# Two mixing blocks on one core: attention with fused maximum, transform in bin pairs, third filter layer kept in SBUF, output projection begun with the gating rows

## The reference

```python
# block 1: 8 query heads of 64, 2 key heads, band of 128 tokens to either side
h = rmsnorm(x, g); q, k, v, g_a, u_p, g_p = split(h @ w_in)
s = where(valid, (q @ k.T) * 64**-0.5 + bias, -1e30)
m = maximum(max(s), sink); p = exp(s - m); p = p / (sum(p) + exp(sink - m))
a = (p @ v) * silu(g_a); p = multiscale_pool(u_p, pool_w) * silu(g_p)
x = x + rmsnorm(concat([a, p]) @ w_out, post_g)
# block 2: a long convolution and a gated spatial unit
h = rms_norm(x, w); hy_in, hy_gate, sg_u, sg_v, sg_gate = split(h @ w_in)
x0, x1, v = split(short_conv(hy_in)); k = hyena_filter(...)  # 3 sine layers, decay, divided by its absolute sum
y_a = x0 * (irfft(rfft(v * x1) * rfft(k)) + v * x1 * skip) * silu(hy_gate)
y_b = spatial_gate(sg_u, sg_v) * silu(sg_gate)
x = x + rms_norm(concat([y_a, y_b]) @ w_out, post_w)
```

## Time and profile before

| | us |
|---|---|
| median of three runs | 3576.2 |
| the profiled execution, its own time | 3573.78 |
| its span in the profile | 3572.0 |
| PE busy | 3248.9 (91%) |
| DVE busy | 2550.0 (71%) |
| ACT busy | 731.7 (20%) |

### The profile page before, as it was taken

The page is one execution under the profiler, slowest core; times in us unless marked ns, Lnnn a source line. Parts: engine busy times, 40 slices in busy tenths (PEclk is TensorE's granted clock), DMA queues, the critical chain, the costliest instruction groups (busy, mean ns, idle before and its releaser), DMA issues. The chain is left out here.

```text
span 3572.0 us, 33998 instructions
## 1 busy us (share of the span) xinstructions
PE 3248.9 (91%) x13506; PEld 2287.5 (64%) x13506; DVE 2550.0 (71%) x2615; ACT 731.7 (20%) x1267; POOL 316.8 (9%) x420
## 2 busy tenths in 40 slices
PE   6999999999995789999999999996798989859999
PEld 3444445664444668777788887874465656657887
DVE  6999993995993687999999999942465656443221
ACT  2000001662221220000111111112342433222110
POOL 3222210001330450000000000000000000000010
PEclk9999999999997999999999999998899999969999
DMA  6555542002448454566455554313102020135331
GB/s 200 146 155 141 145 108 95 7 1 89 155 151 277 157 150 127 158 156 177 144 136 141 139 139 139 99 33 146 49 1 98 13 83 18 65 118 165 94 95 59
DMA packets 210784, 407.99 MB, mean 114 GB/s; under 512 B 20657, under 2 KB 132465, under 8 KB 202561
## 3 DMA queue, kind: packets, MB, share of 16 engines
q1 hardware_dynamic: 190720, 335.00, 30.7%
q0 software_dynamic: 18752, 62.42, 6.8%
q10 hardware_dynamic: 1152, 8.39, 0.6%
HBM read 318.70 MB, written 87.05 MB: 114 GB/s over the span
## 5 line engine op out<-in xcount | busy, mean ns | idle before, releaser
L1535 PE MATMUL PS<-HH,WH 128*128 128x512 f32 x1536 | 607.8, 396 | 35.9 <-DVE WL L1433 16.6
L1537 PE MATMUL PS<-HH,WL 128*128 128x512 f32 x1536 | 604.9, 394 | 0.0
L1536 PE MATMUL PS<-HL,WH 128*128 128x512 f32 x1536 | 600.8, 391 | 0.0
L730 PE MATMUL PS<-M 128*128 128x512 f32 x1152 | 498.9, 595 | 6.3 <-DVE M L567 3.7
L97 DVE SCALAR_TENSOR_TENSOR MF<-MF 128x1024 f32<-128x1024 f32 x315 | 404.2, 1283 | 10.0
L730 PEld LDWEIGHTS PS<-M 128*128 128x128 f32 x1152 | 219.5, 191 | 285.1 <-issue 279.0
L1535 PEld LDWEIGHTS PS<-HH,WH 128*128 128x128 f32 x1536 | 290.4, 189 | 102.8 <-DVE MB L1469 14.1
L1537 PEld LDWEIGHTS PS<-HH,WL 128*128 128x128 f32 x1536 | 289.9, 189 | 65.7
L1536 PEld LDWEIGHTS PS<-HL,WH 128*128 128x128 f32 x1536 | 290.1, 189 | 64.3
L1979 PE MATMUL PS<-M 128*128 128x256 f32 x1024 | 260.0, 398 | 14.1 <-DVE M L1870 8.5
L1979 PEld LDWEIGHTS PS<-M 128*128 128x128 f32 x1024 | 190.8, 191 | 71.2 <-issue 24.9
(11 more groups left out here) (190 smaller groups left out, 4628.0 us busy)
## 6 DMA issues: line engine op xcount, KB each, us to landing
MF<-h_scratch SPq DMA_DIRECT2D x380, 256.0 KB, 4.3
M<-c_feat POOLq DMA_DIRECT2D x194, 256.0 KB, 4.2
MF<-w_in SPq DMA_DIRECT2D x56, 512.0 KB, 4.9
M<-u_scratch SPq DMA_DIRECT2D x16, 1024.0 KB, 4.8
M<-w_in SPq DMA_DIRECT2D x18, 512.0 KB, 5.2
M<-x SPq DMA_DIRECT2D x16, 512.0 KB, 5.5
x_scratch<-M SPq DMA_DIRECT2D x16, 512.0 KB, 2.6
h2h_scratch<-HTH SPq DMA_DIRECT2D x16, 512.0 KB, 2.7
```

The source lines that it names most:

```text
L730: ins = t.matmul(PS[:, banks + c, :], wt[:, k], HT[:, k, TC * c:TC * c + TC], start=(k == 0), stop=(k == KD - 1))
L1535: t.matmul(dst, wh, hh, start=(k == 0), stop=False)
L1536: t.matmul(dst, wh, hl, start=False, stop=False)
L1537: ins = t.matmul(dst, wl, hh, start=False, stop=(k == KD - 1))
```

## The change

In attention the scale moves into the copy of q. Addition of the bias and maximum, the sink's included, become one fused DVE instruction for each of four heads, which order shows as an ISA row and an accumulator read. PE's order becomes: two turns, the value products of the step before (now 256 columns wide, the two halves of the columns in alternation), two turns, the scores. The gate is done a step later. In the mixing loop ACT does the scaling of L658, and 17 of the first layer's operations move ahead of attention. The third layer stays in SBUF (`HP`), its sine is taken on ACT during the second last tiles, constants of the first chunk are loaded ahead, and the second block no longer ends with waits for stores. In the transform a pair of bins is one unit: two matmuls for the inputs and four for the filter in place of eight, three ACT copies, and one DVE product of 1024 columns and one difference of 512. Buffers for decay, absolute values and `GX` are double; the sums come one piece later. Banks 0 to 5 hold the pairs, 6 the inverse, 7 the next filter pieces. The last channel group has its own buffer for `GU`, and `output` starts with rows 8 to 15, whose features and first three weight rows have been loaded before the convolution ends.

```diff
-                    s.activation(Q[:, g], flat, ACT.Copy).then_inc(proj_evac, 1)
+                    s.activation(Q[:, g], flat, ACT.Copy, scale=SCALE).then_inc(proj_evac, 1)
                 elif kind == "k":
...
+                    if st >= 2:
+                        s.wait_ge(pv_done, st - 1)
+                    nk = P * len(keys_of(n))
+                    s.activation(turned_keys(st % 2, r, nk), PS[:, 4 + r % 2, 0:nk], ACT.Copy).then_inc(pT_read, 1)
...
+                s.wait_ge(x1rstd_done, i + 1)
+                s.activation(HS[:, i % 2], X1[:, i % 2], ACT.Copy, scale=RS2[:, i:i + 1]).then_inc(hs_done, 1)
...
-                link_to(v.scalar_tensor_tensor(out=sc, in0=PS[:, 0:4, c0:c1], scalar=SCALE,
-                                               in1=BIAS[:, 4 * g:4 * g + 4, c0:c1], op0=ALU.mult, op1=ALU.add),
-                        scores_read, st + 1)
-                link(v.tensor_reduce(sm[:, 0], sc, AX_X, ALU.max))
-                link(v.tensor_tensor(sm[:, 0], sm[:, 0], SINK[:, 4 * g:4 * g + 4], ALU.max))
+                for r in range(4):
+                    ins = v.tensor_tensor_reduce(out=sc[:, r], in0=PS[:, r, c0:c1], in1=BIAS[:, 4 * g + r, c0:c1], scale=1.0,
+                                                 scalar=SINK[:, 4 * g + r:4 * g + r + 1], op0=ALU.add, op1=ALU.max,
+                                                 accum_out=sm[:, 0, r:r + 1])
+                link_to(ins, scores_read, st + 1)
...
-                if st:
-                    gate(st - 1)
+                if st >= 2:
+                    gate(st - 2)
+            gate(len(STEPS) - 2)
             gate(len(STEPS) - 1)
...
-                first_layer_work(6 if i < 8 else 5)
+                first_layer_work(5 if i < 7 else 4)
...
+                if st:
+                    products(st - 1)
+                turned(2)
+                turned(3)
                 if st + 3 < len(STEPS):
                     scores(st + 3)
+            def products(st):
+                n, g = STEPS[st]
+                ks = keys_of(n)
+                t.wait_ge(pT_read, 4 * st + 4)
                 if st >= 2:
                     t.wait_ge(attn_done, st - 1)
-                product(0)
-                turned(2)
-                product(1)
-                turned(3)
-                product(2)
-                product(3).then_inc(pv_done, 1)
+                for x, kb in enumerate(ks):
+                    for odd in range(2):
+                        ins = t.matmul(PS[HD * odd:HD * odd + HD, 6 + st % 2, 0:2 * P].rearrange("p (a b) -> p a b", b=P),
+                                       V[:, kb, HD * g:HD * g + HD], turned_probs(st % 2, odd, x), start=(x == 0),
+                                       stop=(x == len(ks) - 1))
+                ins.then_inc(pv_done, 1)
             scores(0)
             scores(1)
             scores(2)
             for st in range(len(STEPS)):
                 values(st)
+            products(len(STEPS) - 1)
...
+                for d in range(2):
+                    sp.dma_start(CC[HID * d:HID * d + HID, 0:CH], A["filt_w_out_2"][:, D * d:D * d + CH]).then_inc(kept.first_in, 16)
+                sp.dma_start(CC[:, CH:2 * CH], A["c_delta"][0:CH].partition_broadcast(P)).then_inc(kept.first_in, 16)
+                sp.dma_start(CC[:, 2 * CH:], A["c_tneg"]).then_inc(kept.first_in, 16)
                 a = sum(SV_OPS)
...
-                sp.wait_ge(sin3_done, 1)
-                sp.dma_start(h3_d, L3[2]).then_inc(h3_stored, 16)
-                sp.wait_ge(h3_stored, 16)
-                for b in range(2):
-                    sp.wait_ge(yb_stored[b], 64)
-                sp.wait_ge(gx_stored, 128)
-                sp.wait_ge(u_stored, 128)
...
+                    if (kind, n) == ("hgate", 7):
+                        s.wait_ge(arg3_done, 2)
+                        s.activation(L3[2][0:HID], L3[1][0:HID], ACT.Sin).then_inc(sin3_done, 1)
+                        s.activation(L3[2][HID:P, 1:S], L3[1][HID:P, S - 1:0:-1], ACT.Sin).then_inc(sin3_done, 1)
...
+        DEC = [region(22528 + 512 * i, 512) for i in range(2)]
+        KABS = [region(23552 + 512 * i, 512) for i in range(2)]
...
+        GX = region(37888, 2, S // 2)
...
+        LAST = 2 * NCH - 1
+        GX_LAST = region_of(HP, 0, 2, S // 2)
...
+                if ug == LAST:
+                    sp.wait_ge(utr_done, 4 * LAST + 4)
+                elif ug:
+                    sp.wait_ge(ya_stored[(ug - 1) % 2], 16 * ((ug + 1) // 2))
...
-            sp.dma_start(H3[0:HID], h3_d[0:HID]).then_inc(h3_in, 16)
+                if ug == LAST:
+                    sp.wait_ge(kgen_done, 16 * NCH)
+                elif n >= 2:
+                    sp.wait_ge(gx_used, n - 1)
+                sp.dma_start(gate_part(n), gx_d[ug][:, 1024 * half:1024 * half + 1024]).then_inc(gx_last_in if ug == LAST else gx_in[half], 16)
...
+            sp.wait_ge(ia_done, 4 * (LAST - 1))
+            for b in range(2):
+                sp.wait_ge(kept.yb_stored[b], 64)
+            late_features(sp, YR, yb_d, 1, 0, kept.y_in)
+            late_weights(sp, A, WR, 0, kept.wo_in)
+            late_features(sp, YR, yb_d, 1, 1, kept.y_in)
+            for n in range(1, W_SLOTS):
+                late_weights(sp, A, WR, n, kept.wo_in)
+            sp.dma_start(GP, A["post_norm_w_2"].partition_broadcast(P)).then_inc(kept.gp_in, 16)
+            gated_out(LAST - 1)
+            gated_out(LAST)
+            sp.wait_ge(ya_stored[0], 16 * NCH)
...
-                    s.activation(DEC[:, CH * x:CH * x + CH], DELTA[:, cc % 2], ACT.Exp,
+                    s.activation(DEC[kq % 2][:, CH * x:CH * x + CH], DELTA[cc % 2], ACT.Exp,
...
+                    if 15 * cc + j > 2:
+                        s.wait_ge(kabs_added, 15 * cc + max(j - 2, 0))
+                    s.activation(KABS[j % 2], out, ACT.Abs).then_inc(kabs_done, 1)
...
-                s.activation(UTB[:, n % 16], PS[:, 4 + n % 2, :].rearrange("p (y c) -> p y c", y=2), ACT.Copy).then_inc(z_done, 1)
...
             for kq in range(16):
-                decays(kq)
+                if kq < 15:
+                    decays(kq + 1)
                 absolute(kq)
...
+                for p in range(16):
+                    n = 16 * cc + p
+                    bank = 3 * (n % 2)
+                    s.wait_ge(uk_done, n + 1)
+                    if n >= 2:
+                        s.wait_ge(pm_done, n - 1)
+                    for to in range(2):
+                        s.activation(KS[HID * to:HID * to + HID, n % 2, :, CH:2 * CH],
+                                     PS[HID - HID * to:P - HID * to, bank:bank + 2, 0:CH], ACT.Copy).then_inc(ks_done, 1)
+                    if p == 0:
+                        s.wait_ge(ks_done, ks_count(n) - 2)
+                        s.activation(KS[0:1, n % 2, 0, CH:2 * CH], PS[HID:HID + 1, bank, 0:CH], ACT.Copy,
+                                     scale=-1.0).then_inc(ks_done, 1)
+                    s.wait_ge(b_done, n + 1)
+                    s.activation(KS[:, n % 2, :, 0:CH], PS[:, bank + 2, :].rearrange("p (y c) -> p y c", y=2),
+                                 ACT.Copy).then_inc(ks_done, 1)
+                    if cc + 1 < NCH:
+                        decays(n + 16)
+                    if p:
+                        inverse_out(n - 1)
+                        if cc + 1 < NCH:
+                            absolute(n + 15)
...
+                v.tensor_tensor(out.rearrange("p (c x) -> p x c", x=2), PS[:, sample_bank(kq), :].rearrange("p (x c) -> p x c", x=2),
+                                DEC[kq % 2].rearrange("p (x c) -> p x c", x=2), ALU.mult).then_inc(k_weighted, 1)
...
+                    if n:
+                        v.wait_ge(y_done, n)
+                    v.tensor_tensor(PM, PS[:, bank:bank + 2, :], KS[:, n % 2], ALU.mult).then_inc(pm_done, 1)
+                    v.wait_ge(pm_done, n + 1)
+                    v.tensor_tensor(UTB[:, p], PM[:, :, 0:CH], PM[:, :, CH:2 * CH], ALU.subtract).then_inc(y_done, 1)
+                    if cc + 1 < NCH:
+                        weighted(n + 16)
+                        if p >= 2:
+                            summed(n + 14)
...
+                if kq >= 16:
+                    t.wait_ge(k_weighted, kq)
+                elif kq >= 2:
...
                 bp = n % 16
-                t.wait_ge(y_done, 2 * n + 2)
-                if n >= 2:
-                    t.wait_ge(z_done, n - 1)
...
-                    for m, (strip, which) in enumerate(FORMS):
-                        src = (UTB if which == "u" else KTB[cc % 2])[:, b // 2, b % 2]
-                        ins = t.matmul(PS[:, 2 * (bb % 2) + m // 2, CH * (m % 2):CH * (m % 2) + CH],
-                                       STRIP[:, b, HID * strip:HID * strip + P], src, start=True, stop=True)
+                for p in range(16):
+                    n = 16 * cc + p
+                    bank = 3 * (n % 2)
+                    def form(strip, x, src, at, bank):
```

(45 more changed lines are left out.)

465 lines of the change are left out of this document (228 added, 237 removed).

## The result

The changed kernel takes 3384.86 us (median of four runs, 3380.03 to 3385.71); the kernel before has 3574.84 with the run beside it. The ratio is 0.9465, interval 0.9449 to 0.9482: 190 us less. What follows is about the 21 us by which the parts, 189 us in all, exceed the forecast sum of 168, and about two parts whose size was right for a reason that the prediction did not give.

The account below looks back on a forecast made before the run. PE was taken to bound the kernel almost everywhere, DVE attention. Terms 36 + 4 + 34 + 55 + 18 + 21 = 168 took 3573.8 to 3405.8 us, 3408 as median; range 3385 to 3450, about 8 in 10.

Parts of the forecast that it names:

- The likeliest case: Whole kernel: each part comes out near its forecast value, 3408 us, own range 3385 to 3425; chance 0.60.
- two signs of being wrong: Prediction is wrong if transform pairs have idle PE time or attention's four fused instructions take over 3 us.
- attention: Attention loop: fused instructions and new PE order cut a step from 6.46 to 5.3 us, 36 gained, bounds 26 to 45.
- the start of the convolution: Long convolution's start: stage before ends 6 us sooner, first weighting 11, faster pieces 18; 34 taken, 29 to 38.
- mixing: Mixing loop's end: moved first-layer operations free DVE for L650 (2 us) and the turned tile; 4 us, between 2 and 6.
- rival 2: Attention: products go one half after the other on PE, step 5.6, with handovers 5.75, gain 22, total 3422; chance 0.13.
- rival 1: Attention: fused instruction runs at half rate, near 0.96 us each; attention loses 4 instead of winning 36, total 3448; chance 0.13.
- they gain nothing inside the PE-bound mixing loop: Mixing loop: moving 17 first-layer operations (21 us of DVE work) ahead of attention was claimed to gain nothing inside the loop.
- End: Convolution's end: own GU for the last group saves 10.73, early loads for the last projection 10; 21 us, 15 to 24.
- Pairs and GX: Transform: six matmuls a pair instead of eight, net 55 us (30 to 60); double GX, three transitions, 18 (8 to 22).
- rival 3: Transform: chain PE, ACT, DVE and back bounds the pair at 5.3 us, 22 us more, total 3430; chance 0.12.
- DVE sets the step: Attention before the change: DVE has no gap inside the 6.46 us step while ACT and PE end early, so DVE bounds it.

Follow-up runs that it names:

- e12: Changed kernel with the mixing loop's scaling on DVE again instead of ACT: 270.3 us from mixing's start to the next stage in place of 269.0.
- e11: Changed kernel with the gating features and first three weight rows of the last projection loaded only when that stage begins: 3391.72 us.
- e10: Changed kernel with one buffer for GX again, loads in the order of before: 3399.83 us.
- e2: Kernel before with only the fused instructions and the scale in the copy of q, PE's old order kept: 3571.11 us against 3570.88.
- e3: Changed kernel with one buffer each for decay and absolute values, code order as changed: 3436.37 us.

## Why the prediction came out as it did

The likeliest case was the one that happened, none of the rivals did, and the sum of the convolution's middle and end (-94) met the measured -92.0. Neither of the two signs of being wrong came: the pairs have no idle PE time, and the fused four take 2.27 us. The step that failed is the sizing of three terms: attention (36, measured 43.3), the start of the convolution (34, measured 40.2) and mixing (4, measured 9.9). They came out 19.4 us too small together, of the 21 missing. Term by term:

- *Attention*, 43.3 in place of 36. I took a step of 5.3, between 4.95 and 5.6; it is 5.10. The products are 12 records in 1.44 us (forecast 1.6 if the halves run beside each other, 2.85 if not), so rival 2's condition is absent, and rival 1's too, at 0.61 an instruction where it asked for 0.96. Going halfway to rival 2's value was the error: 4.95 with the same 0.2 for handovers would have been 5.15.
- *Start of the convolution*, 40.2 in place of 34, above my upper 38. The pieces come every 1.32, and the 45.2 us from the first weighting to `filter_first` became 22.1 where I had 27. That ACT bounds them was right, but not its 1.42: in 0.89 + 0.53 I added the decays' length (0.89) to the distance of the absolute value, where the distance of the decays is 0.80. And I took 1.6 rather than the bound, as room for PE at the lower clock; PE's granted clock was 0.50 only in the first 6 us and 1.00 from 2420 us on. The 6 and the 11 us ahead of them were right (6.0 and 11.2).
- *Mixing*, 9.9 in place of 4. The loop's end gave 7.2 (25.0 to 17.8 us from PE's last mixing matmul to DVE's last result), and the loop itself 3.0. The step "they gain nothing inside the PE-bound mixing loop" was wrong by these 3 us. At the loop's end I had 2 for L650; from PE's last mixing matmul it came 4.8 sooner (7.1 to 2.3 us). Of these, 1.8 are POOL's, whose factor I had read as fixed at 1068.2: its two operations took 1.02 and 1.53 us before, with L866 running on DVE, and 0.19 and 0.55 after, with DVE idle; five microseconds later, with L899 on DVE, they took 1.05 and 1.53 again. By `e12` the rest is not the scaling; that it is the 17 moved operations is what remains, and no experiment put them back alone.
- *End*, 21 in place of 21: from the last inverse to the first matmul 30.6 before, 9.6 after. `e11` splits it: 7.6 are the early loads, of the 10 forecast for the start of the projection.
- *Pairs and GX*, 71.0 in place of 73. `e10` gives `GX` 14.8 where I had 18, so the pairs gave about 56 where I had 55.
- 6.7 us came from the second block and the last projection, for which I had nothing, and 3.2 went at the start; much of both is the spread between runs. Against the three terms above, these and the 2 us too many for pairs and `GX` nearly cancel.

The upper bounds of the terms add up to 195 us, which is 3381; the range stopped at 3385, since not all would come out at their better end. They nearly did: attention came out just below its upper bound (45), mixing and the start above theirs (6 and 38). That the median lies 0.14 us outside the range rather than inside is chance: the four runs go from 3380.03 to 3385.71. That the sum was 21 us short is not.

Two mechanisms were not in the prediction. It gave the gain of attention to the fused instruction and asked of PE's new order only how long its loop is; `e2` shows that the old order was itself a ring of 6.4 to 6.6 us, so that "DVE sets the step" was half of the reading. And it priced the buffer of the absolute values at the first 16 pieces alone; `e3` shows that without it rival 3, the chain from ACT to DVE, would have taken back 42 of the pairs' 46 us. The prediction named the chain as a rival, but not that the second buffer is what keeps it away; the old ring it did not name.

## What to carry to other kernels

When an engine is full in a loop, work out the longest ring through the others before pricing a cut: here DVE's row (6.45 us a step with the order changed alone) and PE's ring (6.38 with the instructions changed alone) were nearly equal, and an edit of either alone gained nothing. A buffer that costs nothing now may be what a later cut depends on, so price each part of a change with the others left out. To bound a loop by an engine, add distances from start to start and not lengths, which overlap. And where an engine waits for a load, ask first what stands behind it in its own order: exchanging two calls gained as much (14.7 us) as making the load earlier (13.5).

## What the runs showed of the hardware

- A fused addition and maximum with a scalar, 384 columns from PSUM and SBUF, takes 0.61 us and occupies DVE for 0.54 with its accumulator read of 0.08; half of the 0.16 that I took for the read.
- In these runs 128 matmul records of 64 columns kept PE's clock at the level at which they began: 27.57 us at a granted clock of 0.50, 15.29 at 1.00.
- Twelve records of 256 columns with 64 output rows, which alternate between the two halves, take 1.44 us from the first to the next group, 0.120 each; eight of the same width with 128 output rows take 1.90, 0.238 each. No run has 256 columns and 64 output rows without the alternation.
- POOL's power of one column (L377 before, L388 after) takes 0.55 us with DVE idle and 1.53 with DVE at work on two sources in SBUF.
